# VectorE takes gemm results ahead of the next weights' low part, and two chained norm roots become one joint root

## The reference

```python
hn = rms_norm(h, norm_mlp_g[l])
up = jax.nn.relu(jnp.einsum('bsd,df->bsf', hn, w_mlp_up[l]))      # 1024 -> 4096
h = h + jnp.einsum('bsf,fd->bsd', up * up, w_mlp_down[l])         # 4096 -> 1024
return rms_norm(h, final_norm_g)
```

```python
def swiglu(h, w_gate, w_up, w_down):
    return (jax.nn.silu(h @ w_gate) * (h @ w_up)) @ w_down        # 1024 -> 2816 -> 1024
x = x + 0.5 * swiglu(rms_norm_2(x, ffn1_norm[l]), ffn1_w_gate[l], ffn1_w_up[l], ffn1_w_down[l])
```

## Time and profile before

| | us |
|---|---|
| median of 3 runs | 3655.75 |
| the profiled execution's own time | 3658.47 |
| its span | 3656.6 |
| TensorE matmul busy | 3467.2 (95%) |
| VectorE busy | 1956.3 (54%) |
| ScalarE busy | 1365.6 (37%) |
| mean granted TensorE clock | 0.977 of 2.4 GHz |

### The profile page before, as it was taken

One profiled execution on the slowest core, in us unless ns is written; L12 is line 12 of the kernel. 1 busy time (PEld: TensorE's weight loads), 2 busy tenths in 40 slices (PEclk: granted clock), 3 DMA queues, 4 the chain that ended last, 5 costly groups with the idle time before them and its releaser, 6 DMA issues.

```text
span 3656.6 us, 41944 instructions
## 1 busy us (share of the span) xinstructions
PE 3467.2 (95%) x15516; PEld 2789.5 (76%) x15516; DVE 1956.3 (54%) x2683; ACT 1365.6 (37%) x1914; POOL 213.1 (6%) x158
## 2 busy tenths in 40 slices
PE   7999799899999999999998999999999999999998
PEld 6777577678888788876776888878887777768887
DVE  3677755545445644468643534454435984444434
ACT  3455333432223333345543322242323564342223
POOL 1000000000000000017200000000000550000000
PEclk9999899999999999999999999999999999999999
DMA  4333212223322333322121233333333221213332
GB/s 133 84 90 93 70 35 58 80 82 108 101 94 92 91 93 92 86 84 84 64 81 46 81 101 95 89 95 97 98 89 90 81 78 61 81 47 99 97 92 81
DMA packets 425594, 310.27 MB, mean 85 GB/s; under 512 B 17256, under 2 KB 423200, under 8 KB 425440
## 3 DMA queue, kind: packets, MB, share of 16 engines
q1 hardware_dynamic: 422880, 302.13, 27.7%
q0 software_dynamic: 1664, 4.52, 0.4%
q10 hardware_dynamic: 896, 1.54, 0.1%
HBM read 306.06 MB, written 2.10 MB: 84 GB/s over the span
## 4 chain that ended last, share of the span: by engine, by line
PE 81%; DVE 9%; ACT 5%; issue 4%; DMA 0%; ACTq 0%; DVEq 0%; POOL 0%
PE G L674 72%; ACT w_hi L1122 2%; PE G L800 2%; DVE w_lo L1812 1%; DVE arena L1665 1%; PE G L663 1%; DVE small L1664 1%; DVE y_lo L1827 1%; PE B L663 1%; PE G L619 1%; PE B L540 1%; PE B L581 1%; DVE h L1854 1%; PE B L604 1%; PE B L522 1%
## 5 line engine op out<-in xcount | busy, mean ns | idle before, releaser
L1812 DVE TENSOR_TENSOR w_lo<-raw,w_hi 128x1024 fp32r<-128x1024 f32 x580 | 722.7, 1246 | 1352.7 <-ACT w_hi L1122 1351.8
L674 PE MATMUL G<-xn_hi,w_hi 128*128 128x512 f32 x2864 | 1141.2, 398 | 22.3 <-DVE w_lo L1812 19.4
L674 PE MATMUL G<-xn_hi,w_lo 128*128 128x512 f32 x2864 | 1119.4, 391 | 0.0
L674 PE MATMUL G<-xn_lo,w_hi 128*128 128x512 f32 x2864 | 1118.9, 391 | 0.0
L1122 ACT ACTIVATE w_hi<-raw 128x1024 fp32r<-128x1024 f32 x580 | 613.8, 1058 | 1293.9 <-PE G L674 1272.5
L674 PEld LDWEIGHTS G<-xn_hi,w_hi 128*128 128x128 f32 x2864 | 540.6, 189 | 158.9 <-issue 32.9
L674 PEld LDWEIGHTS G<-xn_lo,w_hi 128*128 128x128 f32 x2864 | 540.5, 189 | 119.7 <-issue 9.9
L674 PEld LDWEIGHTS G<-xn_hi,w_lo 128*128 128x128 f32 x2864 | 539.9, 188 | 113.3
L674 PE MATMUL G<-y_hi,w_hi 128*128 128x512 f32 x1472 | 581.9, 395 | 29.5 <-DVE y_lo L1827 29.5
L674 PE MATMUL G<-y_lo,w_hi 128*128 128x512 f32 x1472 | 578.3, 393 | 0.0
L674 PE MATMUL G<-y_hi,w_lo 128*128 128x512 f32 x1472 | 577.9, 393 | 0.0
(11 more groups left out here) (355 smaller groups left out, 2838.3 us busy)
## 6 DMA issues: line engine op xcount, KB each, us to landing
raw<-in_w_in SPq DMA_DIRECT2D x128, 512.0 KB, 4.5
raw<-in_ffn_w_gate SPq DMA_DIRECT2D x88, 512.0 KB, 4.0
raw<-in_ffn_w_up SPq DMA_DIRECT2D x88, 512.0 KB, 5.2
raw<-in_ffn_w_down SPq DMA_DIRECT2D x64, 512.0 KB, 4.0
raw<-in_w_mlp_up SPq DMA_DIRECT2D x32, 512.0 KB, 4.5
raw<-in_w_mlp_down SPq DMA_DIRECT2D x32, 512.0 KB, 4.0
raw<-in_xa_wkv SPq DMA_DIRECT2D x32, 512.0 KB, 4.4
raw<-in_w_out SPq DMA_DIRECT2D x24, 512.0 KB, 4.3
```

The costliest lines, as they stand in the source:

```text
L674: m = pe.matmul(bank[:, 0:n], a[:, k, kt, :], b[:, kt * S:kt * S + n], start=(kt == 0 and t == 0), stop=(kt == nk - 1 and t == 2))
L1812: dve.tensor_tensor(w_lo[:, k], raw[:, 1 - q, :, k * P:(k + 1) * P], w_hi[:, k].bitcast(F32), ALU.subtract)\
```

## The change

- `residual` and `follow`: h += G comes ahead of w_lo; in `follow` the norm's work of a tile follows in the same step instead of one tile later.
- `swiglu`: except in the first pair after a norm, w_lo of half 1 moves behind G1*rstd and the product with the Silu result, ahead of y_lo.
- `squared_relu`: each half is evacuated and squared as soon as its panel is done; w_lo of half 1 comes behind both (not in the first pair after a norm). ScalarE takes y_hi of half 0 ahead of w_hi of half 1.
- f1u00: `both_vars` makes the argument of one joint root, sum4/D + EPS*var2, before the first w_lo; ScalarE takes this root first and that of the first norm second; `both_rstds` is one reciprocal. The reciprocal of the first norm, which only `normed_h` needs, comes at the end of pair 0.

```diff
             def squared_relu(name, r=None):        # ScalarE
                 def body(i, n, q, landed):
-                    prep(n, q, landed, 0)
-                    if r is not None and isinstance(i, int) and i == 0:
-                        root(r)
-                    prep(n, q, landed, 1)
-                    for k in range(2):
+                    def square(k):
...
+                    first = r is not None and isinstance(i, int) and i == 0
+                    prep(n, q, landed, 0)
+                    if first:
+                        root(r)
+                        prep(n, q, landed, 1)
+                    square(0)
+                    if not first:
+                        prep(n, q, landed, 1)
+                    square(1)
...
                     if name == "f1u00" and isinstance(i, int) and i == 0:
-                        root(2)
                         act.wait_ge(norm_v.sem, norm_v.at("var", 4))
                         act.activation(tmp(4), tmp(4), ACT.Sqrt).then_inc(norm_a.sem, norm_a.mark("std", 4))
+                        root(2)
...
                     for k in range(2):              # VectorE, residual and follow
-                        prep_lo(n, q, k)
                         if k == 0:
                             dve.wait_ge(s_free, n)
                         product(n, k)
...
-                        if j:
-                            norm_tile(r, j - 1, gain, g0)
-                            if more_of:
-                                more_of(j - 1)
-                    if i == 3:
-                        dve.wait_ge(s_free, n + 1)
-                        norm_tile(r, KT - 1, gain, g0)
+                        prep_lo(n, q, k)
+                        if k == 1:
+                            dve.wait_ge(s_free, n + 1)
+                        norm_tile(r, j, gain, g0)
                         if more_of:
-                            more_of(KT - 1)
+                            more_of(j)
...
                     if first:                       # VectorE, squared_relu
                         norm_rstd(r)
-                    prep_lo(n, q, 1)
+                        prep_lo(n, q, 1)
...
-                    for k in range(2):
                         if k == 0:
                             dve.wait_ge(s_ao, i + (BASE[name][0] + 1))
                         else:
                             dve.wait_ge(s_free, n + 1)
                         ins = dve.tensor_tensor(tmp(4 + k), tmp(2 * q + k), tmp(2 * q + k), ALU.mult)
                     squares(ins)
+                    if not first:
+                        prep_lo(n, q, 1)
...
+                    if first and name == "f1u00":   # VectorE, swiglu
+                        both_vars()
                     prep_lo(n, q, 0)
...
-                    prep_lo(n, q, 1)
+                    if first:
+                        prep_lo(n, q, 1)
                     product(n, 1)
                     dve.tensor_tensor(tmp(4 + q), G[2 * q + 1][:, :], rstd[:, :], ALU.mult).then_inc(s_free, 1)
                     dve.wait_ge(s_free, n + 1)
                     dve.wait_ge(s_yh, 2 * i + (BASE[name][1] + 1))
                     dve.tensor_tensor(tmp(2 + q), tmp(4 + q), tmp(q), ALU.mult).then_inc(s_ao, 1)
+                    if not first:
+                        prep_lo(n, q, 1)
...
                     if name == "f1u00":
+                        if first:
+                            norm_rstd(2, S, stat)
                         normed_h(i)
...
+            def both_vars():
+                dve.wait_ge(full.sem, full.at("norm", 4))
+                dve.wait_ge(norm_v.sem, norm_v.at("var", 2))
+                link(dve.tensor_scalar(rstd[:, :], stat[:, :], EPS, None, ALU.mult))
+                dve.scalar_tensor_tensor(tmp(4), B[BANK.get(("norm", 4), 0)][:, :], 1.0 / D, rstd[:, :], ALU.mult, ALU.add)\
+                   .then_inc(norm_v.sem, norm_v.mark("var", 4))
+
             def both_rstds():
-                norm_rstd(2)
-                dve.wait_ge(full.sem, full.at("norm", 4))
-                link(dve.scalar_tensor_tensor(tmp(4), B[BANK.get(("norm", 4), 0)][:, :], 1.0 / D, rstd[:, :], ALU.mult, ALU.mult))
-                link(dve.tensor_tensor(tmp(4), tmp(4), rstd[:, :], ALU.mult))
-                dve.tensor_scalar(tmp(4), tmp(4), EPS, None, ALU.add).then_inc(norm_v.sem, norm_v.mark("var", 4))
-                dve.tensor_copy(stat[:, :], rstd[:, :]).then_inc(norm_v.sem, norm_v.mark("rstd", 2))
                 dve.wait_ge(norm_a.sem, norm_a.at("std", 4))
-                link(dve.reciprocal(tmp(5), tmp(4)))
-                link(dve.tensor_tensor(rstd[:, :], stat[:, :], tmp(5), ALU.mult))
+                link(dve.reciprocal(rstd[:, :], tmp(4)))
```

## The result

The changed kernel takes 3611.84 us (median of 4 runs, 3611.08 to 3617.11) against 3656.09 for the kernel before; ratio 0.9881 with a 95% interval of 0.9868 to 0.9894. Eight runs of it from two comparisons have the median 3614.8. Forecast were 3618.5 us and a range of 3611 to 3634.

What follows compares the result with a forecast made beforehand. TensorE, busy 3467.2 of 3656.6 us, bounds the kernel, so time comes only from its waits and slow stretches. 22.9+4.1+2.8+7.4+0.1 = 37.3 us, giving 3618.5 us against the median; range 3611 to 3634.

Steps and rivals of the forecast that it cites:

- The y_lo waits: Sixteen TensorE waits where up parts end (12 swiglu, 4 squared ReLU) go, except 0.2 us at each six-tile end: 22.9 us.
- T+3.4 and T+3.5: Forecast ends of y_lo after ScalarE sees the panel done (T): T+3.4 in swiglu, T+3.5 for tile 6 in squared ReLU.
- follow (4.1): Where h ends, at nine starts of the next gemm, all xn_lo waits of TensorE go: 4.1 us.
- f1u00 (2.8 and 2.6): In f1u00 the 3.84 us wait for the second w_lo goes, less 1.0 new: 2.8; half-speed matmuls behind it: 2.6 us.
- the new wait of 1.0 us: In f1u00 the moved first-norm reciprocal delays w_lo of half 0 of pair 1: 1.0 us, bounds 0.5 and 2.
- The half-speed stretches: Half-clock matmuls behind waits in f1u00 (2.6) and three of four six-tile ends (4.8) come back: 7.4 us, bounds 0 and 7.6.
- ScalarE in VectorE's place: Rival, 10%: y_hi or the square queued behind w_hi holds y_lo back 1 us more at 12 FFN changes: 3627 us.
- w_lo late in the loops: Rival, 3%: w_lo, now behind two results, becomes late in the 104 pairs of swiglu and squared ReLU: slower, 3671 us.
- a reordering without effect: Rival, 3%: TensorE's waits are really for y_hi or a weight load, only the joint root helps: about 3650 us.
- The clock that stays: Rival, 12%: half-speed stretches belong to the stage changes, not the waits, and remain: 3626 us.
- The six-tile remainder: Wait for y_lo left at the four six-tile swiglu ends: 0.2 us each, or 0.1 by the skill's semaphore rule.

Runs made afterwards that it cites:

- joint root alone: Only the joint root in f1u00 changed against the kernel before, all else as it was: 3650.38 us, ratio 0.9976.
- the version that moves the reciprocal once more: Changed kernel with f1u00's first-norm reciprocal in pair 1's idle time, cmix's result ahead of w_lo, cgate's last reciprocal behind w_lo: 3607.56 us, again 3607.18.
- three kernels: The kernel before (3656.09 us), the same with only squared_relu reordered (3645.13 us), and the same with only f1u00's joint root (3650.38 us).
- h first alone: Against the kernel before, only residual and follow take h += G ahead of w_lo, follow with the norm's work in the same step: 3645.38 us, ratio 0.9974.
- part runs: The kernel before with one part each: residual and follow 3645.38 us, swiglu 3634.82, squared_relu 3645.13, f1u00's joint root 3650.38.
- six-tile run: Swiglu's new order in the six-tile parts only (4 stage changes), all else as the kernel before: 3644.16 us, ratio 0.9970.

## Why the prediction was right, and by how much it was off

**The y_lo waits (22.9 us without the clock).** Right in mechanism and place: all sixteen are gone and w_lo was never late. T+3.4 and T+3.5 were the forecast ends of y_lo, T+3.3 and T+3.2 the measured ones. The term was too small by what lies behind a wait: each cost 0.14 us more than its own length, because the matmuls right behind it are slower or further apart. I had the rows (0.40 instead of 0.39 us drawn) and did not count them. Over the 16 y_lo and 9 xn_lo waits the measured terms are 3.3 us above the forecast ones.

**follow (4.1).** 5.5 measured, for the same reason. VectorE's waiting in line for ScalarE harmed nothing.

**f1u00 (2.8 and 2.6).** Right to 0.1 us, the new wait of 1.0 us for the moved reciprocal included. The joint root alone and the version that moves the reciprocal once more (1.1 us back) both show it.

**The half-speed stretches (7.4).** They came back in the profiled executions as forecast. But to count three of the four as the price of this wait was too firm: with the wait in place three of the four places had a fall in three kernels, and one, the fourth, in h first alone. What the change takes away is the possibility of a fall, 1.6 us each time, not a fixed 4.8 us.

**What no term held (5.7 us of the profiled execution's 45.9).** It lies 2.0 us ahead of the first MLP and 3.4 in mix and cross attention, in stages that no one touched, and 0.3 at the memory's norm in f1d00. In cross attention it is the clock. The same hundred microseconds around cross attention of layer 1, in the kernel before, the changed one, and the changed one once more, have these granted clocks:

```profile
3140.00:3240.00 100.00, 86.29 (x335) 62.10 (x335) 35.45 (x77) 35.22 (x81) 0.00 (x0) 0.91 0.13 43
```

```profile
3104.00:3204.00 100.00, 85.73 (x352) 61.40 (x351) 36.98 (x79) 36.78 (x84) 0.00 (x0) 0.97 0.13 43
```

```profile
3102.00:3202.00 100.00, 85.98 (x340) 61.62 (x339) 36.61 (x79) 36.91 (x84) 0.00 (x0) 0.93 0.13 43
```

0.91, 0.97 and 0.93: the second and third are the same program, and against the kernel before they gain 3.8 and 1.1 us in this stretch. For the 2.0 us ahead of the first MLP the clock is not shown as the cause: its mean over these 832 us is 0.96 before and after. By this the changed kernel's first median of 3611.84 was a lucky one and 3614.8 the better number; against the 3656 of before that is 41 us, 4 more than forecast. I put the effect of clocks elsewhere into the upper end of the range only; it worked downwards.

**The rivals.** ScalarE in VectorE's place, w_lo late in the loops, and a reordering without effect are all excluded by the waits that are left and by the part runs. The clock that stays is excluded by the six-tile run. The rule of the Trainium skill that stood beside it ("TensorE: Matmul & The Clock Gate", section "Why this matters for your kernels") asks for longer gaps; here a fall followed single waits of 2.03 us (once in seven) and 2.28 us (10 times in 16), and the measurement decides. The Trainium skill's page "VectorE: DVE Perf Modes", section "The DRAIN you can't avoid", says that the semaphore costs nothing extra; here the product again started 0.15 us after the multiply's end (1509.06+0.69 to 1509.90), while w_lo at 1510.51, which takes nothing from the product, started 0.08 before the end of the one ahead of it. The six-tile remainder was 0.12 us, near the 0.1 of that rule, but not for its reason: w_lo and y_lo each started 0.08 to 0.09 us before the end of the operation ahead.

## What to carry to other kernels

Where one engine sets the pace, look at the stage changes: there what another engine does *first* in its body is on the path, though in the steady loop the same order is free. Give the result that the next stage waits for precedence over a preparation with slack, and price it from the panel's end (T) on both sides: when each piece ends, and when it is due. For gains of a few microseconds compare the n-th instruction of two traces place by place; two medians of four runs of the same program lay 4 us apart here, and single runs of one program up to 15 us.

## What the runs showed of the hardware

- Between matmuls of this shape 0.227 us at full clock and 0.427 us at half; a wait costs its length plus 0.14 us even when the granted clock stays at 1.00.
- The clock fell behind none of seven waits of 1.48 us, one of seven of 2.03, and 10 of 16 of 2.28 (three of four in three kernels, one of four in another). One fall behind such a wait costs 1.6 us.
- A 128x512 reciprocal on VectorE takes 3.35 us, five times a multiply (0.69). With one instead of two on the way to the second w_lo, a wait of 3.8 us of TensorE became one of 1.0.
- Runs of the same program differ by up to 15 us: the kernel before took 3643.77 to 3659.0 in the 17 runs beside the four part runs, joint root alone 3641.97 to 3653.36.
